# Inverses of 64x64 blocks: transposes as quadrant products beside the level's product, and the second lane of the RWKV scan one step behind

## The reference, cut to what matters

```python
lmat = jnp.where(strict, jnp.einsum('bhncd,bhnsd->bhncs', kb, k) * decay, 0.0)
rhs = jnp.concatenate([vb, kb * jnp.exp(gc)[..., None]], axis=-1)
sol = lax.linalg.triangular_solve(lmat, rhs, left_side=True, lower=True, unit_diagonal=True)
```

```python
sa = jnp.einsum('bhvk,bhk->bhv', S, -kk_t)
S = (S * w_t[:, :, None, :] + sa[..., None] * (kk_t * a_t)[:, :, None, :]
     + v_t[..., None] * k_t[:, :, None, :])
```

## Time and profile before

| what | value |
|---|---|
| median of 3 runs | 3795.48 us |
| lowest, highest | 3793.31, 3803.53 us |
| the profiled execution | 3804.48 us |
| its span | 3803.2 us |
| its mean granted TensorE clock | 0.972 |

### The profile page before, as it was taken

How to read it: one execution, slowest core, us unless ns; L and a number is a source line. 1 busy time by engine, 2 the same in 40 slices (tenths; PEclk the granted TensorE clock), 3 DMA queues, 4 the chain that set the end, 5 groups by cost and what they waited for, 6 DMA issues and landing times.

```text
span 3803.2 us, 72363 instructions
## 1 busy us (share of the span) xinstructions
PE 3532.9 (93%) x31740; PEld 2276.7 (60%) x31740; DVE 1675.3 (44%) x2942; ACT 1181.9 (31%) x2157; POOL 1393.0 (37%) x1239
## 2 busy tenths in 40 slices
PE   7999899999999989898999998999888888889998
PEld 3755584344554555554555554456667677658887
DVE  1245562366531234444333425524666666433344
ACT  3154342322214633413000002114666556320002
POOL 1230550133312245665323333344444444144443
PEclk9999899999999989999999999999999999999999
DMA  5441005311112135301111211331000000122221
GB/s 190 133 137 34 2 14 178 127 47 54 49 49 68 45 111 177 134 23 52 59 56 56 66 51 50 105 112 51 17 17 17 17 17 3 55 70 89 89 89 67
DMA packets 196435, 263.78 MB, mean 69 GB/s; under 512 B 6135, under 2 KB 151671, under 8 KB 194072
## 3 DMA queue, kind: packets, MB, share of 16 engines
q1 hardware_dynamic: 188960, 241.74, 19.2%
q10 hardware_dynamic: 7160, 17.41, 1.2%
HBM read 246.55 MB, written 12.58 MB: 68 GB/s over the span
## 4 chain that ended last, share of the span: by engine, by line
PE 53%; ACT 6%; DVE 4%; issue 4%; POOL 1%; DMA 0%; ACTq 0%; DVEq 0%; SPq 0%; POOLq 0%
PE ps L238 42%; PE ps L3238 2%; PE ps L771 2%; ACT mem L848 1%; PE ps L382 1%; PE ps L798 1%; PE ps L786 1%; PE ps L489 1%; DVE mem L829 1%; PE ps L3757 1%; POOL mem L3540 0%; PE ps L498 0%; PE ps L3765 0%; ACT mem L858 0%; ACT mem L3173 0%
## 5 line engine op out<-in xcount | busy, mean ns | idle before, releaser
L238 PE MATMUL ps<-mem 64*64 64x64 f32 (+4 forms) x25120 | 2624.0, 295 | 98.4 <-ACT mem L3173 26.1
L238 PEld LDWEIGHTS ps<-mem 64*64 64x64 f32 (+1 forms) x25120 | 1704.2, 150 | 1025.4 <-issue 519.6
L3103 POOL TENSOR_TENSOR mem<-mem 128x256 f32<-128x256 f32 (+1 forms) x264 | 228.2, 878 | 342.6 <-ACT mem L3650 176.8
L866 POOL TENSOR_SCALAR mem<-mem 128x768 f32<-128x768 f32 (+2 forms) x128 | 219.3, 1727 | 202.7 <-DVE mem L832 202.7
L2366 ACT ACTIVATE mem<-ps 128x384 f32<-128x384 f32 (+1 forms) x80 | 35.7, 446 | 779.1 <-PE ps L238 736.8
L2353 POOL TENSOR_TENSOR mem<-mem 128x512 f32<-128x512 f32 (+1 forms) x80 | 100.9, 1261 | 445.2 <-PE ps L238 368.4
L596 POOL TENSOR_TENSOR mem<-mem 128x512 f32<-128x512 f32 (+1 forms) x72 | 75.3, 1064 | 417.5 <-ACT mem L591 414.3
L2377 DVE TENSOR_TENSOR mem<-mem,ps 128x384 f32<-128x384 f32 (+1 forms) x80 | 39.9, 499 | 415.8 <-PE ps L238 415.8
L3238 PE MATMUL ps<-mem 128*128 128x128 f32 x960 | 166.4, 289 | 26.6 <-DVE mem L3162 14.0
L3162 DVE TENSOR_TENSOR mem<-mem,ps 128x256 f32<-128x256 f32 (+1 forms) x220 | 109.6, 514 | 110.8 <-PE ps L238 109.9
L3171 ACT ACTIVATE mem<-ps 128x256 f32<-128x256 f32 (+1 forms) x220 | 101.5, 462 | 173.3 <-PE ps L3238 173.0
(11 more groups left out here) (339 smaller groups left out, 4082.7 us busy)
## 6 DMA issues: line engine op xcount, KB each, us to landing
mem<-i_mod_w SPq DMA_DIRECT2D x48, 1024.0 KB, 6.9
mem<-i_ffn_wg SPq DMA_DIRECT2D x22, 1024.0 KB, 5.3
mem<-i_ffn_wu SPq DMA_DIRECT2D x22, 1024.0 KB, 5.3
mem<-i_e_w_in SPq DMA_DIRECT2D x16, 1024.0 KB, 6.2
mem<-i_o_w_in SPq DMA_DIRECT2D x16, 1024.0 KB, 5.4
mem<-i_ffn_wd SPq DMA_DIRECT2D x16, 1024.0 KB, 4.9
mem<-i_e_mod_w SPq DMA_DIRECT2D x12, 1024.0 KB, 11.8
mem<-i_o_mod_w SPq DMA_DIRECT2D x12, 1024.0 KB, 6.6
```

The lines of the kernel that those rows point to most:

```text
L238: ins = e.h.matmul(out, l, r, start=(i == 0), stop=(i == n - 1))
L866: K.pool.h.tensor_scalar(w, w, stat(i, o, 1), None, MUL).then_inc(*nm.up(tag, i, o))
L3103: K.pool.h.tensor_tensor(m3(self.slot(l)), self.lraw, bm(C(K, f"cm{self.d}", l, 64), 2 * self.np), MUL).then_inc(*self.mk.up(key, l))
```

## The change

1. In a level, U is transposed by products of its 64x64 quadrants with a 64x64 identity, 4n of them, into the columns from 256 on of the same banks b and b+1 that take the level's product (`turned`). One copy on ScalarE takes both to one tile PT, of which T and P are halves. Transposes' bank and the wait for it are gone.
2. The delta scan's last step does the same with only the four quadrants it needs; the sign that a copy applied moves to a tile NB = -BE, made by one VectorE instruction ahead of the loop. The gate matmul keeps bank 5 (now GB), the key products move to bank 4 (TB); two steps of VectorE's front shift by one (idle 2 to 1, 5 to 6).
3. In the RWKV scan, lane 1's streams on all four engines begin one step behind lane 0's (`behind`).

```diff
-    RI = [{"U": w[0], "T": w[1], "P": w[2], "Lm": w[3:5]} for w in own]
+    RI = [{"U": w[0], "Lm": w[3:5]} for w in own]
+    for R, m in zip(RI, (held, tail)):
+        R["PT"] = m[:, 256:768]
...
-        vacant(K, FB)
+        vacant(K, TB)
         for h in range(4):
-            ins = K.pe.h.matmul(K.ps[FB][:, HS[h]], kT[:, h, c0:c0 + 128], kT[:, h, c0:c0 + 128], start=True, stop=True)
+            ins = K.pe.h.matmul(K.ps[TB][:, HS[h]], kT[:, h, c0:c0 + 128], kT[:, h, c0:c0 + 128], start=True, stop=True)
...
-        yield from inv.levels(a, TB)
-        vacant(K, TB)
+        yield from inv.levels(a)
+        claim(K, a, inv.cp, inv.key, 6)
         K.pe.wait_ge(*inv.u.at(inv.key, 5))
-        turn(K, K.ps[TB], U, 0, 2).then_inc(*inv.pr.up(inv.key, "v", 6))
-        K.busy[TB] = [(inv.cp, (inv.key, "T", 6))]
-        vacant(K, a)
+        for g in range(2):
+            for h in range(2):
+                w = slice((2 * g + h) * 64, (2 * g + h) * 64 + 64)
+                K.pe.h.matmul(K.ps[a + 1][on(h), on(g)], U[on(q), w], K.id64[on(q), :], start=True, stop=True)
...
-        K.act.h.activation(RI[d]["T"], K.ps[TB][:, 0:256], ACT.Copy).then_inc(*inv.cp.up(inv.key, "T", 6))
         K.act.wait_ge(*inv.pr.at(inv.key, "p", 6))
-        K.act.h.activation(RI[d]["P"][:, 0:128], K.ps[2 * d][:, 0:128], ACT.Copy, scale=-1.0).then_inc(*inv.cp.up(inv.key, "P", 6))
+        K.act.h.activation(h3(inv.P), K.two(2 * d)[:, :, 0:128], ACT.Copy).then_inc(*inv.cp.up(inv.key, 6))
...
+    def turned(self, b):
+
+        return self.K, self.np, BY_EH, by_rows(self.K, b, "heads", 64, 256), (chunky(self.R["U"]), lambda i, e, h: self.id64[64 * e:64 * e + 64, :])
...
         for l in range(1, 6):
-            vacant(K, tb)
+            claim(K, b, self.cp, key, l)
             K.pe.wait_ge(*self.u.at(key, l - 1))
-            turn(K, K.ps[tb], R["U"], 0, self.np).then_inc(*self.pr.up(key, "v", l))
-            K.busy[tb] = [(self.cp, (key, "T", l))]
-            claim(K, b, self.cp, key, "P", l)
+            many(*self.turned(b))
             K.pe.wait_ge(*self.mk.at(key, l))
-            many(K, self.np, BY_EH, by_rows(K, b, "heads"), (chunky(self.slot(l)), chunky(R["U"]))).then_inc(*self.pr.up(key, "p", l))
+            many(K, n, BY_EH, by_rows(K, b, "heads"), (chunky(self.slot(l)), chunky(R["U"]))).then_inc(*self.pr.up(key, "p", l))
             yield
...
-            K.act.wait_ge(*self.pr.at(key, "v", l))
-            K.act.h.activation(self.R["T"][:, 0:self.n], K.ps[turned][:, 0:self.n], ACT.Copy).then_inc(*self.cp.up(key, "T", l))
             K.act.wait_ge(*self.pr.at(key, "p", l))
-            K.act.h.activation(split(self.R["P"], n), both(K, b, n), ACT.Copy).then_inc(*self.cp.up(key, "P", l))
+            out = self.R["PT"][:, 0:n * 256].rearrange("p (a h w) -> p h a w", h=2, w=n * 64)
+            K.act.h.activation(out, K.two(b).rearrange("p h (a w) -> p h a w", w=256)[:, :, :, 0:n * 64], ACT.Copy).then_inc(*self.cp.up(key, l))
...
+def by_half(ap, n):
+
+    return lambda i, e, h: ap[64 * h:64 * h + 64, (e * n + i) * 64:(e * n + i) * 64 + 64]
...
-                streams = ([z(hp - 1)] if hp else []) + ([weave(w(hp, 0), w(hp, 1))] if hp < 8 else []) + ([self.later(f(hp + 1))] if hp < 7 else [])
+                streams = ([z(hp - 1)] if hp else []) + ([weave(w(hp, 0), self.behind(w(hp, 1)))] if hp < 8 else []) + ([self.later(f(hp + 1))] if hp < 7 else [])
                 run(*streams)
         self.loads()
+
+    def behind(self, lane):
+
+        yield
+        yield from lane
```

More of the change, by code:

```diff
@@ L1359, in delta_scan @@
     held = K.ring.slots[K.ring.slot(first + 2)]
-    own = [[m[:, i * 256:(i + 1) * 256] for i in range(7)] for m in (held, K.alloc(1792))]
+    tail = K.alloc(1792)
+    own = [[m[:, i * 256:(i + 1) * 256] for i in range(7)] for m in (held, tail)]
     more = [K.alloc(512) for _ in range(2)]
-    RI = [{"U": w[0], "T": w[1], "P": w[2], "Lm": w[3:5]} for w in own]
+    RI = [{"U": w[0], "Lm": w[3:5]} for w in own]
+    for R, m in zip(RI, (held, tail)):
+        R["PT"] = m[:, 256:768]
     Lc, Lo, OD = [(own[d][5], more[d][:, 0:256]) for d in range(2)], [(own[d][6], more[d][:, 256:512]) for d in range(2)], ot[:, 4:8, :]
@@ L1392, in front_pe @@
         tt, x, c0 = place(d, i)
[L1393 removed]
+        vacant(K, GB)
         K.pe.wait_ge(*gate.at(d, i))
[L1395 to L1396 removed]
+        K.pe.h.matmul(K.ps[GB], C(K, "ones"), gm[d], start=True, stop=True).then_inc(*pr.up(d, i, "gate"))
+        K.busy[GB] = [(ux, (d, i, "x"))] + ([(ex, (d, i, "qs"))] if x else [])
         yield from idle(2)
[L1398 removed]
+        vacant(K, TB)
         for h in range(4):
[L1400 removed]
+            ins = K.pe.h.matmul(K.ps[TB][:, HS[h]], kT[:, h, c0:c0 + 128], kT[:, h, c0:c0 + 128], start=True, stop=True)
         ins.then_inc(*pr.up(d, i, "kk"))
[L1402 removed]
+        K.busy[TB] = [(ux, (d, i, "L"))]
         yield from idle(6)
@@ L1419, in front_dve @@
             K.dve.h.tensor_tensor(h3(qs[d][i % 2]), h3(qs[d][i % 2]), qT[:, :, c0:c0 + 128], MUL).then_inc(*ux.up(d, i, "qs"))
-        yield from idle(2)
+        yield from idle(1)
         K.dve.wait_ge(*pr.at(d, i, "kk"))
@@ L1428, in front_dve @@
         for e in range(2):
-            K.dve.h.tensor_tensor(m3(Lc[d][i % 2])[on(e)], part(K.ps[FB], e, e), part(E, e, e), MUL).then_inc(*ux.up(d, i, "L", e))
-        K.dve.h.tensor_tensor(m3(Lo[d][i % 2])[on(s)], part(K.ps[FB], s, q), part(E, s, q), MUL).then_inc(*ux.up(d, i, "L"))
-        yield from idle(5)
+            K.dve.h.tensor_tensor(m3(Lc[d][i % 2])[on(e)], part(K.ps[TB], e, e), part(E, e, e), MUL).then_inc(*ux.up(d, i, "L", e))
+        K.dve.h.tensor_tensor(m3(Lo[d][i % 2])[on(s)], part(K.ps[TB], s, q), part(E, s, q), MUL).then_inc(*ux.up(d, i, "L"))
+        yield from idle(6)
         if x:
@@ L1444, in front_act @@
                 K.act.wait_ge(*ch.at(d, i - 2, "o"))
-            K.act.h.activation(qs[d][i % 2], K.ps[FB], ACT.Exp).then_inc(*ex.up(d, i, "qs"))
+            K.act.h.activation(qs[d][i % 2], K.ps[GB], ACT.Exp).then_inc(*ex.up(d, i, "qs"))
         yield
@@ L1494, in inverse_pe @@
         ins.then_inc(*inv.pr.up(inv.key, "p", 6))
-        K.busy[a] = [(inv.cp, (inv.key, "P", 6))]
         yield
         claim(K, a, ux, d, i, "off")
-        K.pe.wait_ge(*inv.cp.at(inv.key, "P", 6))
+        K.pe.wait_ge(*inv.cp.at(inv.key, 6))
         for g in range(2):
             for h in range(2):
-                ins = K.pe.h.matmul(K.ps[a + h][on(q), on(g)], T[on(h), (2 * g + q) * 64:(2 * g + q) * 64 + 64], P[on(h), on(g)], start=True, stop=True)
+                ins = K.pe.h.matmul(K.ps[a + h][on(q), on(g)], inv.P[on(h), 128 + 64 * g:192 + 64 * g], inv.P[on(h), on(g)], start=True, stop=True)
         ins.then_inc(*inv.pr.up(inv.key, "u", 6))
@@ L3079, with __init__ @@
 class Inverse64:
-    def __init__(self, K, key, before, R, lane, d, lraw, np_, id64, first=None, turned=None):
+    def __init__(self, K, key, before, R, lane, d, lraw, np_, id64, first=None):
         self.K, self.key, self.before, self.R, self.lane, self.d = K, key, before, R, lane, d
-        self.fb, self.tb = first, turned
+        self.fb = first
+        self.P, self.T = (R["PT"][:, j * np_ * 128:(j + 1) * np_ * 128] for j in range(2))
         self.lraw, self.np, self.n, self.id64 = lraw, np_, np_ * 128, id64
@@ L3133, in pe @@
         yield from self.first(b + 1)
-        yield from self.levels(b, b + 2)
+        yield from self.levels(b)
     def pool(self, ready):
```

28 lines of the change are left out of this document (14 added, 14 removed).

## The result

The changed kernel took 3906.39 us (median of 4 runs, 3899.55 to 3908.63) against 3796.27 us: a ratio of 1.0284, 95% interval 1.0264 to 1.0304. It is slower by 110 us. The forecast of 3797 us, with a range up to 3827 us, is wrong, and so is its likeliest case, no change.

The account below looks back on a forecast made before the run. TensorE was taken as the bound: its slots in the delta scan, copies, updates and 128-record instruction blocks in the RWKV scan. Terms -9 + 21 - 9.6 - 5 + 4 = +1.4 us on 3795.48 gave 3797 us, range 3774 to 3827.

Parts of the forecast that it names:

- its likeliest case, no change: Whole kernel: time within about 0.3% (11.4 us) of the kernel before, chance 0.41.
- One lane a step behind: RWKV scan: lane 1's lag saves 5 us after each pass's last product in all, costs 4 us before n=4 levels.
- The clock (rival 3): RWKV levels at n=4: TensorE's idle time draws the clock to 1.2 GHz, +32 us, 3829 us; chance 0.12.
- The sign I had named: RWKV passes: a granted clock below 0.9 would show that idle time in the levels slows TensorE's clock.
- The other terms, -9 + 21 - 9.6: Delta scan -9 us, RWKV levels at n=4 to the pass's end +21 us, RWKV levels at n=2 -9.6 us.
- Levels at n=4 by the fetch: RWKV scan: added records make instruction blocks limit a level of both lanes to 5.2 us; +21 us in all.
- not over 80: RWKV scan: stalls named "issue" were to total over 80 us against 18.9, as a sign of the fetch limit.
- Levels at n=2: RWKV scan: TensorE's slots save time in five levels per pass, fetch binding only in single levels; -9.6 us over eight passes.
- Delta scan: Delta scan, 12 units: shorter TensorE slots save 0.8 us per unit; -9 us taken, ends -20 and +6.
- The wait for L3721: RWKV scan, after a pass's last product: this 6.5 us wait goes as lane 1's products lie between; -5 us.
- Rival 1: RWKV levels: instruction fetch does not bind, n=4 levels take 3.7 us, -12 instead of +21, 3764 us; chance 0.10.
- The rule that the prediction set beside it: TensorE, from the Trainium skill: issue pace hides fetching and the buffer holds 2048 instructions, so added records cost nothing themselves.

Follow-up runs that it names:

- e1_no_lag: The changed kernel with both lanes of the RWKV scan in the same step again; 3833.01 us, ratio 1.0083.
- e2_lag_only: The kernel before with only lane 1 of the RWKV scan one step behind, transposes and two copies as they were; 3896.99 us, ratio 1.0252.
- e10_lag_both_later: e2_lag_only with the next pair's front and the finish of the pair before each one step later; 3818.40 us, ratio 1.0047.
- e3_joint_turn: e1_no_lag with true 128x128 transposes kept in the levels, written to the product's banks, still one wide copy; 3824.25 us, ratio 1.0057.
- e11_no_turns: e1_no_lag with the quadrant transposes at n=4 left out in levels 2 to 5, part of the computation missing; one run, 3817.68 us.
- e5_dummies: e3_joint_turn with 14 small unread products of 8 columns added per lane and level at n=4; 3870.91 us, ratio 1.0184.

## Why the prediction was wrong, point by point

- **One lane a step behind: this step failed.** The forecast put it at -5 + 4 = -1 us. It is +97 us alone. I had followed the lag into one place, the turned copies ahead of the n=4 levels, and sized it at 0.6 us a pass; the longest wait there went from 1.5 us to 3.7 us, and that stretch grew by 21 us in eight passes (147.1 to 168.2). I had not followed it into the other streams. The waits for the level's copy went from 20.6 to 36.0 us, those for the nb product behind `sol` from 0.7 to 25.5 us, and the n=2 levels, which share their steps with the finish, from 170.1 to 191.0 us. Shifting front and finish by one step took 79 us back: what costs is for the most part the place of lane 1 against its neighbour streams, and not the lag between the lanes. How much of the cost belongs to which wait stays open, and so do the last 19 us. None of my rivals was about the lag.
- **The clock (rival 3): right in kind, in another place, and it had no term in the sum.** I had sought it in the idle time of the new n=4 levels. There `e1_no_lag` kept its full clock nearly throughout (3.4 of their 228.5 us at 1.2 GHz). But with the waits that the lag brings it fell: `e2_lag_only` has 85.3 us of the scan at 1.2 GHz for 6.8, which is some 39 of the 97 us, and with most of these waits gone `e10_lag_both_later` has 17.1. The mean over the whole kernel, 0.966 against 0.972 in the changed kernel, hides this, as it takes in all other stages. The sign I had named, a granted clock below 0.9 in the passes, was not reached: it was 0.95.
- **The rest of the sum was off too.** The other terms, -9 + 21 - 9.6, came to +2.4 us; without the lag `e1_no_lag` is 33 us slower. The 31 us between are the three points that follow. By themselves they would have put the time at 3829 us, just outside the range. (TensorE's idle share in the four scan windows of the earlier trace rows was 7 to 22%, not 10 to 20%.)
- **Levels at n=4 by the fetch, +21 us: right in kind, too small.** Without the lag the levels and what follows went from 343.1 to 378.9 us (203.6 + 139.5, 228.5 + 150.4), +36 us, at 5.2 to 5.6 us a level in the last pass for 5.2 forecast. But `e3_joint_turn`, with no added records in its levels, has 9 us of that too, from the wide copy, which I had covered by the other lane; at n=4 it lies open for 0.42 us a level. Some of the 36 us is the clock as well: behind the levels `e1_no_lag` has 27.3 us at 1.2 GHz, the kernel before 6.8. In the changed kernel's last pass two levels take 11.5 us (3366.73 to 3378.24), and its issue stalls came to 15.2 us in all, not over 80.
- **Levels at n=2, -9.6 us: right in sign, too large.** It is -3.1 us in `e1_no_lag`. The count beside it was wrong: 140 records are added per pass (five levels, two lanes, 14 each), not about 104; the sum does not use it.
- **Delta scan, -9 us: it gained nothing, because of a wait I had not looked for.** I counted what leaving bank TB would win and did not ask who newly shares it. The slots saved were real: -0.9 us a unit with the old banks, where -0.8 was forecast.
- **The wait for L3721** fell by 2.5 us and did not go away, where -5 us was forecast. A wait of 11.1 us for the read of `ps` (L3723) came beside it, 0.8 us before (L3709).
- **Rival 1** (the fetch does not bind) is refuted by the 49 stalls of `e1_no_lag`, which come at multiples of 128 records, and by `e11_no_turns`, where they all but leave the levels with the added records. The rule that the prediction set beside it does not hold for these dense quadrant products.

## What to carry to other kernels

Where every engine runs one hand-ordered stream, moving one lane by a step moves it against every other stream woven in; walk each engine's order past the table loads and the wide operations of those streams before calling a shift free, and try shifting them along with it. Read the granted clock over the changed stage and not over the kernel: where TensorE's busy time grows with the same products, part of the loss is the clock. When a tile moves to another PSUM bank, list who now shares that bank, not only who left it. Count TensorE's instructions as well as its time when transposes are replaced by many small products.

## What the runs showed of the hardware that I had not expected

The stalls named "issue" came up in the mixed stretches of the levels as well, not only in the densest ones: `e1_no_lag` had 49 of them, 46.2 us; where two of them stand one block of 128 records apart, they end 3.39 to 4.02 us apart. A single wait of 3.7 us was followed by a granted clock of 0.50 (`e2_lag_only`, from 3053 to 3056 us). Over the scan such stretches came to 85.3 us in that kernel for 6.8 before, and TensorE was busy for 38.8 us more with the same products. And a small float32 product of 64x8 held TensorE for some 0.028 us per record (26 records from 3330.02 to 3330.76 us in `e5_dummies`, by their start to the start of what follows), twice the 0.0147 us at which records of 64x64 in all four quadrants follow each other; these small ones used only two of the quadrants, and no run tells whether that or their width is the reason.

```profile
3329.43 0.66 PE L3129 MATMUL ps<-mem 128*128 128x128 f32 x4
3330.02 0.93 PE L3134 MATMUL ps<-mem 64*64 64x8 f32 x26
3330.76 0.27 PE L238 MATMUL ps<-mem 64*64 64x64 f32 x2
```
